# The even mixer of a two-block model: pool products in two steps, two output slots in rooms of their own, one head scaled by ScalarE

## What is computed

```python
def even_mixer(h, w_in, w_out, q_g, k_g, pool_w, pool_scale):
    proj = h @ w_in
    q, k, v, qi, ki, wi, u = jnp.split(proj, offsets, axis=-1)
    q = rms_norm_2(q.reshape(b, t, A_HEADS, HEAD_DIM), q_g)
    k = rms_norm_2(k.reshape(b, t, A_KV_HEADS, HEAD_DIM), k_g)
    attn = dsa_attention(q, k, v, qi, ki, wi)
    pooled = multiscale_pool(u, pool_w, pool_scale)
    return jnp.concatenate([attn, pooled], axis=-1) @ w_out
```

## Time and profile before

| | |
|---|---|
| median of three runs | 1362.8 us (1358.01 to 1365.09) |
| the profiled execution, its own time | 1359.04 us |
| its span, first to last instruction | 1357.3 us |
| mean granted TensorE clock | 0.992 |
| busy: PE, DVE, ACT, POOL | 96%, 48%, 50%, 75% |
| HBM read | 213.26 MB, 159 GB/s over the span |

### The profile page before, as it was taken

One profiled execution on the slowest core, in us unless ns is written; L12 is line 12 of the kernel. 1 busy time (PEld: TensorE's weight loads), 2 busy tenths in 40 slices (PEclk: granted clock), 3 DMA queues, 4 the chain that ended last, 5 costly groups with the idle time before them and its releaser, 6 DMA issues.

```text
span 1357.3 us, 27756 instructions
## 1 busy us (share of the span) xinstructions
PE 1306.6 (96%) x11024; PEld 1257.2 (93%) x11024; DVE 656.8 (48%) x1168; ACT 674.5 (50%) x925; POOL 1014.5 (75%) x794
## 2 busy tenths in 40 slices
PE   6989999999999999999999979999999999999999
PEld 6879999999988888999998958999999998999999
DVE  8994465555555757555555574211113545211112
ACT  7715544444666755444456446433346445544442
POOL 1226898888777649888878866888887664888885
PEclk9999999999999999999999989999999999999999
DMA  6313675555535335555544422555554432555530
GB/s 262 126 63 126 179 245 179 178 178 183 184 132 182 110 109 195 186 180 178 177 177 165 175 97 94 187 187 185 185 184 151 144 120 94 184 187 181 180 136 31
DMA packets 33880, 217.07 MB, mean 160 GB/s; under 512 B 3684, under 2 KB 7429, under 8 KB 8197
## 3 DMA queue, kind: packets, MB, share of 16 engines
q1 hardware_dynamic: 30096, 211.14, 44.4%
q10 hardware_dynamic: 3700, 4.75, 1.4%
HBM read 213.26 MB, written 2.62 MB: 159 GB/s over the span
## 4 chain that ended last, share of the span: by engine, by line
PE 81%; DVE 10%; ACT 4%; POOL 2%; issue 2%; DMA 1%; DVEq 0%; ACTq 0%; SPq 0%; POOLq 0%
PE up L1491 18%; PE up L1492 18%; PE up L1493 18%; PE acc L1491 6%; PE acc L1493 6%; PE acc L1492 6%; PE up L1611 1%; POOL w_lo L388 1%; ACT w_hi L469 1%; DVE opnd L888 1%; DVE s_work L1028 1%; PE side L1697 1%; DVE mix L897 1%; DVE s_work L1037 1%; DVE mix L1369 1%
## 5 line engine op out<-in xcount | busy, mean ns | idle before, releaser
L388 POOL TENSOR_TENSOR w_lo<-ring,w_hi 128x512 fp32r<-128x512 f32 x756 | 971.4, 1318 | 237.4 <-ACT w_hi L469 235.3
L1491 PE MATMUL up<-opnd,w_hi 128*128 128x256 f32 x2128 | 612.6, 288 | 11.5 <-POOL w_lo L388 4.6
L1492 PE MATMUL up<-opnd,w_lo 128*128 128x256 f32 x2128 | 603.2, 283 | 0.0
L1493 PE MATMUL up<-opnd,w_hi 128*128 128x256 f32 x2128 | 603.1, 283 | 0.0
L469 ACT ACTIVATE w_hi<-ring 128x2048 fp32r<-128x2048 f32 x191 | 364.5, 1910 | 264.9 <-PE up L1493 211.2
L1491 PEld LDWEIGHTS up<-opnd,w_hi 128*128 128x128 f32 x2128 | 409.0, 192 | 25.1 <-issue 17.2
L1492 PEld LDWEIGHTS up<-opnd,w_lo 128*128 128x128 f32 x2128 | 409.2, 192 | 1.2 <-issue 1.0
L1493 PEld LDWEIGHTS up<-opnd,w_hi 128*128 128x128 f32 x2128 | 409.2, 192 | 0.0
L1491 PE MATMUL acc<-opnd,w_hi 128*128 128x256 f32 x768 | 217.8, 284 | 2.6 <-DVE opnd L1129 2.6
L1492 PE MATMUL acc<-opnd,w_lo 128*128 128x256 f32 x768 | 217.3, 283 | 0.0
L1493 PE MATMUL acc<-opnd,w_hi 128*128 128x256 f32 x768 | 217.3, 283 | 0.0
(11 more groups left out here) (286 smaller groups left out, 1378.3 us busy)
## 6 DMA issues: line engine op xcount, KB each, us to landing
ring<-in_stream SPq DMA_DIRECT2D x197, 1024.0 KB, 4.9
bias_rows<-mix ACTq DMA_DIRECT2D x1, 1536.0 KB
mix<-in_s_b SPq DMA_DIRECT2D x1, 1024.0 KB, 6.2
x<-in_x SPq DMA_DIRECT2D x1, 1024.0 KB, 8.2
mix<-in_s_c SPq DMA_DIRECT2D x1, 1024.0 KB, 12.2
mix<-bias_rows ACTq DMA_DIRECT2D x1, 1024.0 KB, 5.3
out_x<-x SPq DMA_DIRECT2D x8, 128.0 KB, 1.7
mix<-in_p ACTq DMA_DIRECT2D x2, 256.0 KB, 4.4
```

The source lines that it names most:

```text
L388: ins = nc.gpsimd.tensor_tensor(w_l[:, cols], ring[:, r, cols], w_h[:, cols].bitcast(f32), ALU.subtract)
L1491: MM(o, l_hi, r_hi, start=start, stop=False, skip_group_check=True)
L1492: MM(o, l_lo, r_hi, start=False, stop=False, skip_group_check=True)
L1493: return MM(o, l_hi, r_lo, start=False, stop=stop, skip_group_check=True)
```

## The change

Pool: the subtraction of u leaves POOL. ScalarE writes the negated pool weights into a free buffer (`e_pwn`); TensorE adds up two products per group, -pool_w with u in step 0 and pool_w with the window means in step 1. ScalarE's four pool copies move to step 1, VectorE's four lows to step 2, all together.

Rooms: the second and the fourth output slot (`evout` 1 and 3) get rooms of their own in `mix`, so the high part of each waits for other things than a free place: for the norms that read what lies there, and for a pool product. The first slot of ffn2 then has its place free early, and its high part stands in step 5. The fourth slot's products go into the bank acc[:, 0], its tiles 4 to 7 in step 9 and 0 to 3 in step 12.

Head 1: the second tensor_scalar of a unit goes to ScalarE (`even_scaled`), which waits for `sum_inv`; the logits two units later wait for it (`probs_e1`), and so do the transposes.

Norms: the Exp of a norm goes back into its PSUM bank, and VectorE's product reads it there.

Order on TensorE: the first output part stands in step 3 with four tiles; from step 8 on the transposes and values stand ahead of the step's output parts.

```diff
@@ buffers
+        e_room = (TT * P + 5 * T + 16 * T + 2 * T + 64)
+        e_pwn = e_at[:, 0].rearrange("p (g d) -> p g d", g=4)
-        last_hi = {START["wo"] + 3: mix_r[:, 0:2048], START["evout"] + 3: mix_r[:, 512:2560]}
+        last_hi = {START["wo"] + 3: mix_r[:, 0:2048], START["evout"] + 1: mix_r[:, e_room:e_room + 2048],
+                   START["evout"] + 3: mix_r[:, e_room + 2048:e_room + 4096]}
...
@@ gpsimd
+                if s == START["evout"] + 1:
+                    pool.wait_ge(sem("pooled"), 4)
...
                 c.up(nc.gpsimd.tensor_tensor(e_cnt[:, g], e_cnt[:, g], (e_pa if g % 2 else e_pb)[:, g, 16:], ALU.mult),
-                     "pool_step")
-            pool.wait_ge(sem("pool_step"), c.of("pool_step").value())
-            c.up(nc.gpsimd.tensor_tensor(e_cnt, e_cnt, e_u[:, :, 16:], ALU.subtract), "pooled")
+                     "pooled")
@@ scalar
+                elif s == START["evout"] + 1:
+                    act.wait_ge(sem("qk_ready"), 8 + 2)
                 elif s == START["evout"] + 3:
-                    act.wait_ge(sem("scores"), 8)
+                    act.wait_ge(sem("pool_ps"), 1)
+                    act.wait_ge(sem("qk_ready"), 8 + 3)
+                elif s == START["ffn2"]:
+                    act.wait_ge(sem("mm_done"), START["evout"])
...
-                c.up(A(b, b, ACT.Exp, scale=-0.5), "hn_rstd")
+                c.up(A(aux[n % 2], b, ACT.Exp, scale=-0.5), "hn_rstd")
...
+            def even_scaled(n):
+                c.wait("sum_inv")
+                e = 1
+                nk, b = P * (n % 2 + 1), n % 2
+                L = e_l[:, b].rearrange("p (c k) -> p c k", c=2)[:, e, 0:nk]
+                c.up(A(e_a[:, b].rearrange("p (c k) -> p c k", c=2)[:, e, 0:nk], L, ACT.Copy,
+                       scale=e_st[:, 48 + 2 * b + e:49 + 2 * b + e]), "probs_e1")
...
-            high_parts_to(S + 8)
+            act.wait_ge(dma["causal"], 48)
+            c.up(A(e_pwn, e_pw, ACT.Copy, scale=-1.0), "pool_neg")
+            high_parts_to(S + 7)
             even_square(1)
             even_root(1)
             even_square(2)
-            high_parts_to(S + 9)
             for n in range(EVEN_STEPS):
-                if n == 3:
-                    c.wait("pool_ps", 4)
+                if 2 <= n < 10:
+                    even_probs_copy(n - 2)
+                if 2 <= n <= 8:
+                    even_scaled(n - 1)
+                if n < 8:
+                    softmax_exp(n, e_l, e_st)
+                if n == 0:
+                    high_parts_to(S + 8)
+                if n == 1:
+                    even_scaled(0)
+                    c.wait("pool_ps")
                     for m in range(4):
                         c.up(A(hi("mixed")[:, 4 + m], up[(BANK["evout"] + m // 2) % 2][:, m % 2], ACT.Copy,
                                scale=pcol("pscale", m, 1)), "hi_ready")
-                if 2 <= n < 10:
-                    even_probs_copy(n - 2)
-                if n < 8:
-                    softmax_exp(n, e_l, e_st)
-                if n == 1:
                     even_root(2)
+                    high_parts_to(S + 9)
                 if n >= 5 and n % 2:
...
-                if n == 9:
+                if n == 3:
                     high_parts_to(S + 10)
+                if n == 5:
+                    high_parts_to(S + 11)
@@ vector
+                if n >= 2:
+                    dve.wait_ge(sem("probs_e1"), n - 1)
...
+            def even_probs(n):
+                nk, b = P * (n % 2 + 1), n % 2
+                L = e_l[:, b].rearrange("p (c k) -> p c k", c=2)[:, 0, 0:nk]
+                c.wait("exps", 2)
+                r = e_st[:, 48 + 2 * b:50 + 2 * b]
+                c.up_and_wait(V.reciprocal(r, e_st[:, 44 + 2 * b:46 + 2 * b]), "sum_inv")
+                if n >= 2:
+                    c.wait("at_ps")
+                c.up_and_wait(V.tensor_scalar(e_a[:, b, 0:nk], L, r[:, 0:1], None, ALU.mult), "probs")
...
-                if 1 <= n <= 8:
-                    softmax_tail(n - 1, e_l, e_a, e_st, False)
                 if n == 2:
-                    even_normed(2)
-                if n in (3, 4):
-                    c.wait("hi_ready", 2)
-                    for m in (2 * n - 6, 2 * n - 5):
+                    c.wait("hi_ready", 4)
+                    for m in range(4):
...
+                if 1 <= n <= 8:
+                    even_probs(n - 1)
+                if n == 2:
+                    even_normed(2)
...
-            residual("ffn2", START["evout"], BANK["evout"], {2: acc[:, 3]})
+            residual("ffn2", START["evout"], BANK["evout"], {2: acc[:, 3], 3: acc[:, 0]})
@@ tensor
-            fill = {4: [(0, [4, 5])], 5: [(0, [6, 7])], 6: [(1, [4, 5])], 7: [(1, [6, 7])], 8: [(0, [0]), (1, [0])],
-                    9: [(2, [4, 5, 6, 7])], 10: [(0, [1]), (1, [1]), (2, [0, 1])], 11: [(0, [2]), (1, [2]), (2, [2])],
-                    12: [(0, [3]), (1, [3]), (2, [3])]}
+            fill = {3: [(0, [4, 5, 6, 7])], 4: [(1, [4, 5])], 5: [(1, [6, 7])], 6: [(2, [4, 5])], 7: [(2, [6, 7])]}
+            late = {8: [(0, [0]), (1, [0]), (2, [0])], 9: [(3, [4, 5, 6, 7])], 10: [(0, [1]), (1, [1]), (2, [1])],
+                    11: [(0, [2]), (1, [2]), (2, [2])], 12: [(0, [3]), (1, [3]), (2, [3]), (3, [0, 1, 2, 3])]}
...
+            for n in range(EVEN_STEPS):
+                if n < 8:
+                    even_scores(n)
                 if n == 0:
+                    banks = {0: bank(), 1: bank()}
+                    pe.wait_ge(sem("pool_in"), 2)
+                    c.wait("pool_neg")
+                    pool_part(e_pwn, lambda m: e_u[:, m, 16:], True)
+                if n == 1:
                     even_stats(2)
+                    c.wait("pooled", 4)
+                    c.up(pool_part(e_pw, lambda m: e_cnt[:, m], False), "pool_ps")
+                out_parts(fill.get(n, []))
                 if 2 <= n < 10:
                     even_transposes(n - 2)
                 if 4 <= n <= 10 and n % 2 == 0:
                     even_values((n - 4) // 2)
...
+                out_parts(late.get(n, []))
-            up_slot("mixed", out + 3)
```

More of the change, by code:

```diff
@@ L289, in program @@
         d_oh = d_sq.rearrange("p a b -> p (a b)")[0:33, 0:384 + HEADS]
[L290 to L294, removed]
+        (e_v, e_k, e_q, e_l, e_a, e_at, e_mask, e_st, e_causal, e_pl, e_tmp, e_sq, e_half, e_w, e_rel, e_m8, e_cnt,
+         e_pw, e_u, e_pa, e_pb) = carve(
+            (TT, P), (T,), (4, T), (2, 2 * T), (2, 2 * T), (4, 2 * T), (2, T), (64,), (2, T), (3, T), (3, 2 * T),
+            (2, 2 * T), (P,), (TT, 4), (T,), (8,), (4, T), (4, P), (4, 16 + T), (4, 16 + T), (4, 16 + T))
+        e_room = (TT * P + 5 * T + 16 * T + 2 * T + 64)
+        e_pwn = e_at[:, 0].rearrange("p (g d) -> p g d", g=4)
         (k_k, k_q, k_v, k_mask, k_tri, k_z, k_t, k_b, k_a, k_out) = carve(
             (KT, T), (KT, T), (TT, D), (384,), (P,), (3, 768), (2, 768), (2, 768), (2, 768), (2, T))
-        last_hi = {START["wo"] + 3: mix_r[:, 0:2048], START["evout"] + 3: mix_r[:, 512:2560]}
-        last_lo = {START["wo"] + 3: mix_r[:, 6144:8192], START["evout"] + 3: mix_r[:, 2560:4608]}
+        last_hi = {START["wo"] + 3: mix_r[:, 0:2048], START["evout"] + 1: mix_r[:, e_room:e_room + 2048],
+                   START["evout"] + 3: mix_r[:, e_room + 2048:e_room + 4096]}
+        last_lo = {START["wo"] + 3: mix_r[:, 6144:8192], START["evout"] + 1: mix_r[:, e_room + 6992:e_room + 9040],
+                   START["evout"] + 3: mix_r[:, e_room + 4240:e_room + 6288]}
         def weights_hi(s):
@@ L1217, in head_raw @@
                 c.tell("hn_raw")
[L1219 to L1236, removed]
             pe_operand()
@@ L1338, in even_normed @@
                 src = e_tmp[:, n % 3].rearrange("p (a t) -> p a t", a=2)
-                bc = e_sq[:, n % 2].rearrange("p (a t) -> p a t", a=2)
+                bc = aux[n % 2].rearrange("p (a t) -> p a t", a=2)
                 if n == 0:
@@ L1912, in even_stats @@
                 if n == 2:
-                    c.wait("hn_ln")
+                    pe.wait_ge(sem("qk_ready"), 8 + 1)
                 c.up(MM(aux[n % 2], e_half, e_sq[:, n % 2], start=True, stop=True, skip_group_check=True), "hn_ssq")
@@ L1952, in even_transposes @@
                 c.wait("probs")
+                c.wait("probs_e1")
                 if n:
@@ L1964, in even_values @@
                 if h == 0:
-                    c.wait("hn_ln", 2)
+                    pe.wait_ge(sem("qk_ready"), 8 + 3)
                 if h >= 2:
@@ L1978, in _, with pool_part, out_parts @@
             out = START["evout"]
-            fill = {4: [(0, [4, 5])], 5: [(0, [6, 7])], 6: [(1, [4, 5])], 7: [(1, [6, 7])], 8: [(0, [0]), (1, [0])],
-                    9: [(2, [4, 5, 6, 7])], 10: [(0, [1]), (1, [1]), (2, [0, 1])], 11: [(0, [2]), (1, [2]), (2, [2])],
-                    12: [(0, [3]), (1, [3]), (2, [3])]}
-            for n in range(EVEN_STEPS):
-                if n < 8:
-                    even_scores(n)
```

(20 more changed lines are left out.)

6 lines of the change are left out of this document (4 added, 2 removed).

## The result

Four executions of the changed kernel have a median of 1351.04 us (1347.64 to 1353.41), four of the kernel before 1362.45 (1358.01 to 1365.09): a ratio of 0.9914, 95% interval 0.9894 to 0.9934. The change makes the kernel faster. The forecast was 7.0 us less and held no measurable change for slightly likelier than a gain (0.49 against 0.46).

A forecast was written before the change was run, and what follows sets the result against it. TensorE, busy 96% of the span, was taken as the bound. In the even mixer, work 44.3+1.7 and waits 7.2 without half rate gave 53.2 against 59.5; the walk's 7.0 off 1362.8 gave 1355.8 us, range 1351 to 1361.5.

The forecast's parts named there:

- The walk through the stretch: Step-by-step times from the last input slot's end to ffn2's second slot: ends at 837.8 instead of 844.9, gain 7.0.
- The ledger: Sum over the even mixer's stretch: work 44.3+1.7, waits 7.2, no half rate, 53.2 against 59.5 us; gain 6.3.
- tile 6 at the border: Passage to ffn2: VectorE's low 6 there 11.0 us after output part 0, where TensorE wants it at 9.6.
- the norms in PSUM: Head norms: VectorE's product reading PSUM takes 0.7 against 1.12, gaining 0.4 us ahead of the first scores.
- The half rate: TensorE's half clock in the even mixer costs 4.1 us (1.7 pool products, 1.3 twelve matmuls, 1.1 three groups) and goes.
- the second pool product: TensorE, steps 0 and 1: four more f32 products, +1.72 us of work at full rate, filling holes.
- (c): Rival: TensorE's clock still falls; one fall costs 1.7, two 4.1; gain 4 in the middle, 1358.8; chance 0.14.
- forecast case: The main outcome for the whole kernel: a gain of 5.5 to 8.5 us; chance 0.42.
- (b): Rival: queues fit better, transposes 6 wait 1.05, border costs 1, small waits vanish; gain 10, 1352.8; chance 0.18.
- (a): Rival: five head-0 products on VectorE beside POOL, 0.9 us longer each, take 4.5 in all: 1360.3; chance 0.10.
- (e): Rival: output still waits for its pool parts, transposes 1 to 6 wait 0.8 each; gain 2, 1360.8; chance 0.10.
- (d): Rival: slower, the loop of transposes, copy, scaling, exponentials and product closes each step, 5.4 us: 1370; chance 0.06.

The follow-up runs named there:

- the kernel before, kept busy: Kernel before with five unread f32 products on TensorE where it stood still, two in step 2 and three in step 4: ratio 0.9986, stretch 57.2 us.
- one product: Changed kernel with POOL's subtraction back, no negation on ScalarE and one pool product per group: ratio 0.9948, stretch 52.4 us.
- one product, kept busy: Changed kernel with POOL's subtraction, one pool product per group, and two unread f32 products in steps 0 and 3: ratio 0.9933, stretch 51.3 us.
- parts first: Changed kernel with the late output parts of step 8 put ahead of transposes 6 and values 2: ratio 0.9928, stretch 50.9 us.

## Why the prediction was right or wrong

**The walk through the stretch was right.** It gave 7.0 us, measured are 7.7. Its times are those of the kernel before; taken back by the 2.2 us of the start, the first output part was forecast for 792.3 and started at 792.27, transposes 6 for 809.3 and started at 808.68, part 0's end for 822.1 and came at 821.3, and from there to ffn2's second slot I had 13.5 against 13.6. The two clearest signs named, a wait ahead of the first output part and one ahead of the seventh transposes, released by VectorE's lows and ScalarE's scaling, are both there.

**Terms of the sum that were mis-sized.** The ledger had 7.2 of waits, the profile has 4.4: 0.5 for the bank (0.4 forecast), 0.9 for the pool lows (1.4), none ahead of transposes 1 (0.3), 0.4 of small ones (0.8), 1.1 (1.4), and at the border 1.0+0.5 (2.9). Most of it is tile 6 at the border, a wait of 1.4 in the sum and of 0.2 in the run. I had TensorE ask for it 9.6 us behind part 0's end; the first square sums stand ahead of it (829.79 to 830.36), and TensorE asked at 10.6. The low was there at 10.6 too, not at 11.0; it took 0.50, and only low 7 took 1.25. My sum also left out the small gaps, 0.7 in the ledger of the kernel before. With 46.0 of work and 4.4 of waits it would be at 50.4, and the stretch is 51.8, so the ledger errs by 2.8 one way and by 1.4 the other. The 0.4 for the norms in PSUM were no gain.

**The half rate.** It went, as forecast, but its price of 4.1 was that of the matmuls alone; kept warm, the kernel before gains 2.3. By the ledger the 7.7 are 6.0 less of waits and 4.1 less of half rate, with 1.7 more work and 0.7 more of gaps. As causes the first two are not apart, since 1.7 of the half rate lay where TensorE would have waited for VectorE anyway. I had also taken the second pool product for a mere cost (+1.72) that fills holes. It is at the same time, as far as the profiles show, what keeps the clock up: with one product the clock fell at the first output part, and the stretch was 0.6 longer in spite of the saved work. Rival (c) was thus nearer than its text knew, only not in the two profiles of this kernel.

**What failed is the step from the time to the chances.** Measurably faster had 0.46 and no measurable change 0.49, and the outcome is outside the second, by both measurements. The step has two faults. The first is the bound: I took 0.5%, 6.8 us, for what a measurement of this kernel can tell from no change. The intervals are 0.20% to either side (2.7 us) with four executions of each kernel and 0.13% (1.8 us) with 6 and 23, and even the 1.9 us of the kernel before, kept busy, are told apart. With a bound of 2.7 the whole forecast case, (b) and (c), with its gain of 4, are faster: 0.74 by the chances that I gave. The second is the waits counted high. With a forecast of 7.0 beside a bound of 6.8 every tenth mattered, and I put a third of the forecast case's weight below that bound.

Rivals (a), (c) and (e) had a third of all chance, and none came true. (a) Four of the eight head-0 products took 1.2 to 1.3 beside POOL, the size that the rule of the Trainium skill, SBUF — State Buffer, "SBUF: two separate sides", leads to, but none of them released TensorE in this kernel (in one product, kept busy, and in parts first one did, after waits of 1.3 and 0.4). The trace agrees with that rule further than I had used it:

```profile
799.95 5.08 POOL L393 TENSOR_TENSOR mix_r<-ring,mix_r 128x512 fp32r<-128x512 f32 x4 [0.56 <-ACT mix_r L477]
802.24 0.35 DVE L1406 TENSOR_SCALAR mix<-mix 128x128 f32<-128x128 f32 x1
803.99 1.19 DVE L1406 TENSOR_SCALAR mix<-mix 128x256 f32<-128x256 f32 x1
```

The second of these four POOL instructions ends as the third starts, at 802.47, and the last ends at 805.03. The two products end at 802.59 and 805.18, and all eight end 0.10 to 0.15 us behind the end of a POOL instruction. So a product beside POOL costs what is left of POOL's instruction, 0.3 to 1.3 us in all, and my 0.9 more for each was only its upper part. (c) The clock is 1.00 through the stretch in both profiles. (e) The pool parts took their places and one wait of 0.9 was left. (d), slower, needed a loop of over 4.5 us a step and found 2.9. (b), a better fit, was nearer to the truth in its waits.

**Outside of the stretch.** The forecast had nothing there, and nothing of the change is shown there. The first pair of profiles has 2.2 us from the start and 1.5 from the odd mixer's clock on top. The measured 11.4 between the medians and the 8.8 of the second occasion (0.65% of 1358) are 7.7 and such shares. The base was high as well: I started from 1362.8, the median of three executions, and on the other occasions the kernel before has medians of 1358.2 to 1359.1. Less 7.0 that is 1351.2 to 1352.1, against the 1355.8 that I forecast. The median of 1351.04 lies at the very edge of the range, 1351 to 1361.5, for these two reasons, and that it lies inside is luck.

## What to carry to other kernels

Read a stretch between two landmarks that both kernels pass before explaining a difference of whole times: here the stretch repeats within 0.2 us, while whole executions of one kernel differ by up to 7. Where TensorE is the bound and its waits are spread out, see that the first operand of the next stage has a place of its own once little work stands ahead of it (without it this kernel is 5.2 us longer), and look for cheap cover for the waits that remain: moving parts already there into them gave 0.9 and 1.4 us. Before taking work away from a half-idle TensorE, ask what its clock will do. And take the bound for "no measurable change" from the interval of such measurements: here a bound more than twice too wide put no measurable change ahead of a gain that the walk had right.

## What the runs showed of the hardware

A wait of 2.2 us in the odd mixer, whose code is the same in all 14 profiled executions, had the clock at half rate behind it in seven of them and not in the other seven, for 1.5 us (read in six of the seven). A kernel with less work for TensorE ran longer, 52.4 against 51.8 us in the stretch, with its clock at 0.52 for 3 us; two products that nobody reads made it 51.3 with a full clock. The head-0 tensor_scalar on VectorE (128x128 or 128x256) took 0.30 to 1.34 us beside POOL's low parts, by how much of POOL's instruction was left, and ended 0.10 to 0.15 us behind it all eight times.
